# Five modulation units of a two-layer diffusion backbone, moved from TensorE to VectorE dot products

## The reference

```
sh1_l, sc1_l, g1_l, sh2_l, sc2_l, g2_l = split(silu(c)     @ w_ada + b_ada, 6)
sh1_c, sc1_c, g1_c, sh2_c, sc2_c, g2_c = split(silu(c_ctx) @ w_ada + b_ada, 6)
h  = rms_norm(x, norm1_g) * (1 + sc1) + sh1
... = h @ w_in          # attention (a), conformer convolution, differential attention (d), three gates
y  = sigmoid(g0) * (o_mla @ w_o_mla) + sigmoid(g1) * (o_conv @ w_o_conv) + sigmoid(g2) * (o_diff @ w_o_diff)
x  = x + g1 * (y @ w_out)
h2 = rms_norm(x, norm2_g) * (1 + sc2) + sh2
x  = x + g2 * hier_moe(h2)
```

## Time and profile before

| what | us |
|---|---|
| three runs | 1578.43, 1573.87, 1580.1 (median 1578.43) |
| profiled execution, its own time | 1578.7 |
| span from first to last instruction | 1576.9 |
| TensorE busy | 1469.0 (93%) |
| VectorE busy | 629.4 (40%) |
| ScalarE busy | 385.1 (24%) |
| GpSimd busy | 143.1 (9%) |
| mean granted TensorE clock | 0.975 of full speed |

### The profile page before, as it was taken

The page is one execution under the profiler, slowest core; times in us unless marked ns, Lnnn a source line. Parts: engine busy times, 40 slices in busy tenths (PEclk is TensorE's granted clock), DMA queues, the critical chain, the costliest instruction groups (busy, mean ns, idle before and its releaser), DMA issues.

```text
span 1576.9 us, 19712 instructions
## 1 busy us (share of the span) xinstructions
PE 1469.0 (93%) x7940; PEld 825.3 (52%) x7940; DVE 629.4 (40%) x1461; ACT 385.1 (24%) x827; POOL 143.1 (9%) x104
## 2 busy tenths in 40 slices
PE   5999999999999999989997879999999999899886
PEld 3443344454445445565553447644768876555552
DVE  2468943533234202433211117794543214233223
ACT  4111404432222102222221124231542203011111
POOL 0001510000002010002221110051000110000000
PEclk9999999999999999999999899999999999899998
DMA  9422422112221306089999988452212538699994
GB/s 382 178 107 111 190 107 107 54 54 107 104 110 63 163 41 271 37 325 416 418 418 420 411 308 360 194 213 107 101 60 107 218 130 334 262 420 420 420 418 195
DMA packets 49038, 349.23 MB, mean 221 GB/s; under 512 B 7968, under 2 KB 8480, under 8 KB 17328
## 3 DMA queue, kind: packets, MB, share of 16 engines
q1 hardware_dynamic: 43344, 337.42, 53.0%
q0 software_dynamic: 5024, 8.40, 1.4%
q10 hardware_dynamic: 576, 2.10, 0.3%
HBM read 345.00 MB, written 11.80 MB: 226 GB/s over the span
## 4 chain that ended last, share of the span: by engine, by line
PE 80%; DMA 9%; DVE 4%; SPq 3%; ACT 3%; issue 1%; DVEq 0%; POOLq 0%; ACTq 0%
PE bank L358 76%; DMA arena<-w_up_in 7%; ACT arena L1089 2%; PE bank L647 2%; SPq L2425 1%; SPq L2436 1%; DVE arena L1501 1%; PE bank L432 1%; DMA arena<-w_down_in 1%; DMA arena<-ada_in 1%; SPq L2445 1%; PE bank L984 1%; DMA x<-x_in 0%; DVE arena L1745 0%; DMA arena<-y 0%
## 5 line engine op out<-in xcount | busy, mean ns | idle before, releaser
L358 PE MATMUL bank<-arena 128*128 128x512 f32 (+10 forms) x6104 | 1272.6, 453 | 53.9 <-DMA arena<-w_up_in 22.0
L358 PEld LDWEIGHTS bank<-arena 128*128 128x128 f32 (+4 forms) x6104 | 671.0, 162 | 568.0 <-issue 411.1
L1089 ACT ACTIVATE arena<-bank 128x512 f32<-128x512 f32 (+5 forms) x454 | 221.1, 504 | 1014.7 <-PE bank L358 902.3
L1501 DVE SCALAR_TENSOR_TENSOR arena<-arena,bank 64x256 f32<-64x256 f32 (+2 forms) x121 | 58.0, 480 | 436.6 <-ACT arena L1089 267.7
L1501 DVE SCALAR_TENSOR_TENSOR arena<-arena,vec 128x512 f32<-128x512 f32 (+1 forms) x254 | 173.4, 755 | 0.4
L1763 DVE TENSOR_REDUCE am<-bank 128x1 f32<-128x512 f32 (+1 forms) x96 | 55.5, 599 | 181.1 <-PE bank L358 181.1
L2292 POOL TENSOR_TENSOR arena<-arena 128x512 f32<-128x512 f32 (+1 forms) x32 | 31.9, 997 | 551.7 <-DVE arena L1501 551.7
L1089 ACT ACTIVATE arena<-bank,am 128x512 f32<-128x512 f32 (+1 forms) x96 | 58.6, 613 | 73.1 <-DVE am L1766 73.0
L2331 POOL DMA_INDIRECT y<-arena,routing x33 | 33.4, 1013 | 188.5 <-ACT arena L1089 183.5
L358 PE MATMUL bank<-arena,silz 128*32 128x512 f32 x384 | 46.1, 598 | 4.3 <-DMA arena<-ada_in 4.3
L647 PEld LDWEIGHTS bank<-con,arena 128*128 128x128 f32 x240 | 29.3, 141 | 36.7 <-issue 23.6
(11 more groups left out here) (177 smaller groups left out, 672.8 us busy)
## 6 DMA issues: line engine op xcount, KB each, us to landing
arena<-w_down_in SPq DMA_DIRECT2D x65, 1024.0 KB
arena<-w_gate_in SPq DMA_DIRECT2D x61, 1024.0 KB
arena<-w_up_in SPq DMA_DIRECT2D x61, 1024.0 KB
arena<-ada_in SPq DMA_DIRECT2D x24, 2048.0 KB, 8.4
arena<-mg_in SPq DMA_DIRECT2D x12, 2048.0 KB, 7.8
arena<-mo_in SPq DMA_DIRECT2D x6, 2048.0 KB, 8.2
arena<-glu_in SPq DMA_DIRECT2D x4, 2048.0 KB, 12.8
arena<-out_w_in SPq DMA_DIRECT2D x4, 2048.0 KB, 15.1
```

The source lines that it names most:

```text
L358: return nc.tensor.matmul(out, w, rhs, start=start, stop=stop)
L1089: return nc.scalar.activation(out, in_, fn, **kw)
L1501: return V.scalar_tensor_tensor(out, in0, sc, in1, op0=op0, op1=op1)
```

## The change

The five units that stood among the gates and branches of layer 0 leave the ring and TensorE. Their weights come transposed (`adaT`: 128 output columns on the partitions, 1024 inputs along the row), in ten halves of 1 MB. The halves go by turns to two areas outside the ring: that of the convolution output `cv` and that of the values `vd`. VectorE multiplies each with rows of the activations and sums along the row, four products of 128x1024 to a half. The activation rows are loaded once, spread over 128 partitions, and made into silu by a tanh on ScalarE and a product on VectorE.

Half 0 stands before the wait for `dn`, halves 1 and 2 behind the reciprocal, and the other seven each before a branch tile of the last branch, c = 2 left out. A half's load waits until the half two places ahead of it is done. The last two loads stand behind those of the output weights, and the first expert load behind the last half. ScalarE's copies of g1 wait for the last branch, as they overwrite `vd`.

Also, the first differential unit's merge steps are divided in both layers: 4 of them in layer 0 and 8 in layer 1 come on TensorE before the first `turn`. VectorE's and ScalarE's order stays there.

```
-                if kind not in ("mg0", "mg1", "mg4", "mo2"):
+                if kind not in (("mg0", "mg1", "mg4", "mo2") if l else ("mg0", "mg1", "mo0", "mg2", "mg3", "mo1", "mg4", "mo2", "mg5")):
...
+                row_units = more[:ROW_UNITS]
+                del more[:ROW_UNITS]
...
+                AHEAD = (4, 8)[l]
+                def merge_steps(g, part=None):
+                    r0, r1 = merge_range(l, g)
+                    if part is not None:
+                        r0, r1 = ((r0, r0 + AHEAD), (r0 + AHEAD, r1))[part]
...
                 for u in range(len(DU)):
+                    if u == 0:
+                        merge_steps(len(AU), 0)
                     turn(len(AU) + u, dprob(u)[:, 0], DU[u][2])
...
-                    merge_steps(len(AU) + u)
+                    merge_steps(len(AU) + u, None if u else 1)
...
+                        elif l == 0 and (what, b, c) == ("branch", 0, KD - 1):
+                            act.wait_ge(full["d"], Dn[("branch", l, KD - 1, 0)])
+                            act.wait_ge(rows_loaded, 16)
+                            f(tanh_rows, silu_rows, ACT.Tanh, scale=0.5).then_inc(rows_tanh, 1)
...
+                def ada_half():
+                    i = len(half_done)
+                    la, u, hh = halves[i]
+                    w = grid(half_at[i % 2], 2)
+                    dve.wait_ge(half_ready[i % 2], 16 * (i // 2 + 1))
+                    for m in range(2):
+                        c_ = 4 * u + 2 * hh + m
+                        if product_at[0]:
+                            dve.wait_ge(dve_step, product_at[0])
+                        V.scalar_tensor_tensor(product, w[:, m, :], 1.0, silu_rows[:, 0, :], op0=MUL, op1=MUL,
+                                               accum_out=ada[la][:, c_, 0:1]).then_inc(dve_step, 1)
...
+                        ins = V.scalar_tensor_tensor(w[:, m, :], w[:, m, :], 1.0, silu_rows[:, 1, :], op0=MUL, op1=MUL,
+                                                     accum_out=ada[la][:, c_, 1:2])
...
+                    step(ins)
+                    stt(ada[la][:, c_:c_ + 2, :], ada[la][:, c_:c_ + 2, :], 0.5,
+                        vec_at(la, "b_ada")[:, c_:c_ + 2].unsqueeze(2).to_broadcast([128, 2, 2]), MUL, ADD).then_inc(dve_step, 1)
...
+                    if l == 0 and u == 1:
+                        dve.wait_ge(rows_tanh, 1)
+                        step(stt(silu_rows, tanh_rows, 1.0, silu_rows, ADD, MUL))
...
+                if l == 0:
+                    dve.wait_ge(s["pt_ready"], len(AU) + len(DU))
+                    dve.wait_ge(s["pv_full"], len(AU) // 2 + len(DU))
+                    ada_half()
                 dve.wait_ge(empty["a"], A[("dn", l)])
                 V.reciprocal(P[:, 0, q0:T], P[:, 0, q0:T]).then_inc(s["recip_ready"], 1)
+                if l == 0:
+                    ada_half()
+                    ada_half()
...
                 for c in range(KD):
+                    if l == 0 and c != 2:
+                        ada_half()
                     branch(2, c)
...
+            def half_load(i):
+                if i == 0:
+                    sp.wait_ge(dve_step, silu_done[0])
+                elif i == 1:
+                    sp.wait_ge(S[0]["pv_full"], len(attn_units(0)[0]) // 2 + len(attn_units(0)[1]))
+                else:
+                    sp.wait_ge(dve_step, half_done[i - 2])
+                sp.dma_start(half_at[i % 2], a["adaT"][la, u, hh]).then_inc(half_ready[i % 2], 16)
...
+                    if units[n] == ("mg3", 0, 0):
+                        sp.wait_ge(s["conv_out"], CT)
+                        sp.dma_start(silu_rows..., a["crow"].to_broadcast([128, 2 * D])).then_inc(rows_loaded, 16)
+                    if units[n] == ("mo2", 0, 0):
+                        half_load(0)
```

More of the change, by code:

```diff
@@ L28 @@
 NRING = 3
+ROW_UNITS = 5
 NADA = 12
@@ L197, in build @@
         consts_set = sem("consts_set")
+        rows_loaded, rows_tanh = sem("silu_rows_loaded"), sem("silu_rows_tanh")
+        half_ready = [sem(f"ada_half_ready{b}") for b in range(2)]
         silc_tanh, silc_ready = sem("silc_tanh"), sem("silc_ready")
@@ L300, in build @@
         ring_of = [[(n_ - 3 + i_) % NRING for i_ in range(3)] for n_ in (units_of_0, len(units))]
+        halves = [(la, u, hh) for _, la, u in row_units for hh in range(2)]
+        half_at = [cv.rearrange("p c t -> p (c t)"), vd.rearrange("p c t -> p (c t)")]
+        silu_rows = arena[:, 24816:26864].rearrange("p (v k) -> p v k", v=2)
+        tanh_rows = arena[:, 18672:20720].rearrange("p (v k) -> p v k", v=2)
+        product = PT.rearrange("p c t -> p (c t)")
+        half_done, silu_done = [], []
         def ada_behind(key):
@@ L601, in branch_step @@
                             used((f"mo{b}", l, 0), "d")
-                def merge_steps(g):
-                    for r_ in range(*merge_range(l, g)):
+                AHEAD = (4, 8)[l]
[3 more added lines that the diff above has]
+                        r0, r1 = ((r0, r0 + AHEAD), (r0 + AHEAD, r1))[part]
+                    for r_ in range(r0, r1):
                         b, r = divmod(r_, ALL)
@@ L1130, in row_copies @@
             def row_copies(l, kind, tokens):
+                if (l, kind) == (0, "g1"):
+                    act.wait_ge(empty["d"], Dn[("branch", 0, KD - 1, 2)])
                 for v in tokens:
@@ L1522, in scales @@
             def scales(l, which):
-                dve.wait_ge(empty["d"], max(Dn[("adaT", l, u)] for u in {0: (0, 1, 2, 3), 1: (8, 9), 2: (4, 5)}[which]))
+                for u in {0: (0, 1, 2, 3), 1: (8, 9), 2: (4, 5)}[which]:
+                    if ("ada", l, u) in row_units:
+                        dve.wait_ge(dve_step, half_done[halves.index((l, u, 1))])
+                    else:
+                        dve.wait_ge(empty["d"], Dn[("adaT", l, u)])
                 if which == 2:
@@ L1807, in branch @@
                     give(stt(out, out, 1.0, ps[:, 0:NQ], ADD, MUL))
+                def ada_half():
[9 more added lines that the diff above has]
+                                               accum_out=ada[la][:, c_, 0:1]).then_inc(dve_step, 1)
+                        own[0] += 1
+                        product_at[0] = own[0]
+                        ins = V.scalar_tensor_tensor(w[:, m, :], w[:, m, :], 1.0, silu_rows[:, 1, :], op0=MUL, op1=MUL,
+                                                     accum_out=ada[la][:, c_, 1:2])
+                        if m == 0:
+                            ins.then_inc(dve_step, 1)
+                            own[0] += 1
+                    step(ins)
+                    c_ = 4 * u + 2 * hh
+                    stt(ada[la][:, c_:c_ + 2, :], ada[la][:, c_:c_ + 2, :], 0.5,
+                        vec_at(la, "b_ada")[:, c_:c_ + 2].unsqueeze(2).to_broadcast([128, 2, 2]), MUL, ADD).then_inc(dve_step, 1)
+                    own[0] += 1
+                    half_done.append(own[0])
+                product_at = [0]
                 def merge_tiles(g):
@@ L1839, in _ @@
                     merge_tiles(nA + u)
+                    if l == 0 and u == 1:
+                        dve.wait_ge(rows_tanh, 1)
+                        step(stt(silu_rows, tanh_rows, 1.0, silu_rows, ADD, MUL))
+                        silu_done.append(own[0])
                 out_d(len(DU) - 1)
+                if l == 0:
+                    dve.wait_ge(s["pt_ready"], len(AU) + len(DU))
+                    dve.wait_ge(s["pv_full"], len(AU) // 2 + len(DU))
+                    ada_half()
                 dve.wait_ge(empty["a"], A[("dn", l)])
                 V.reciprocal(P[:, 0, q0:T], P[:, 0, q0:T]).then_inc(s["recip_ready"], 1)
+                if l == 0:
+                    ada_half()
+                    ada_half()
                 for i in range(HD):
@@ L1851, in _ @@
                 for c in range(KD):
+                    if l == 0 and c != 2:
+                        ada_half()
                     branch(2, c)
+                assert len(half_done) == len(halves)
                 ada_finish(("mg5", l, 0))
@@ L2410, in _ @@
                         sp.dma_start(wr, a["router"][0]).then_inc(router_loaded, 16)
+                if l == 0:
+                    for i in range(1, len(halves) - 2):
+                        half_load(i)
                 b_last = Dn[("branch", l, KD - 1, 1)]
@@ L2420, in _ @@
                 sp.dma_start(outw[1].rearrange("p k n -> p (k n)"), a["out_w"][l, 1]).then_inc(s["outw_ready1"], 16)
+                if l == 0:
+                    half_load(len(halves) - 2)
+                    half_load(len(halves) - 1)
+                    sp.wait_ge(dve_step, half_done[-1])
                 def expert_quarters(j, pairs, quarters):
@@ L2611 @@
         "ada": flat(rows(w_ada, KD).reshape(L, 128, KD, NADA, 4, 4, 32).transpose(0, 3, 1, 2, 5, 4, 6), 3),
+        "adaT": flat(A(w_ada).transpose(0, 2, 1).reshape(L, NADA, 2, 2, 128, D).transpose(0, 1, 2, 4, 3, 5), 4),
```

(1 more changed line is left out.)

1 line of the change is left out of this document (added).

## The result

| | before | changed |
|---|---|---|
| median of the runs, us | 1578.06 | 1556.24 |
| lowest to highest | 1573.87 to 1580.1 | 1555.49 to 1556.8 |
| profiled execution, its own time / span | 1578.7 / 1576.9 | 1556.7 / 1554.7 |
| mean granted clock | 0.975 | 0.979 |
| VectorE busy | 629.4 | 683.4 |

A forecast was written before the change was run, and what follows sets the result against it. TensorE was taken as the bound, the path for 80% of the span, with room on VectorE. 12.58 + 1.81 + 1.23 - 0.49 = 15.1 us off 1578.4 gave 1563.5 us, range 1557 to 1574.

The forecast's parts named there:

- The units on TensorE: Layer 0: five modulation units leave TensorE, priced by the starts around them; 12.58 us won.
- Nothing on the path for VectorE: Layer 0: VectorE's ten halves fit in its idle time; cost on the path 0.
- The rooms: Layer 0, before branch 0 of the last branch: cover for VectorE's work is gone from 7.0 us a half.
- The size of a half: VectorE, layer 0: four dot products plus a small scale-and-bias take 5.8 us, bounds 5.3 and 10.5.
- Half rate: Rival: layer 0's VectorE products take 2.35 to 2.56 us each, VectorE bounds, 1586 to 1594 us; chance 0.07.
- The transfers: Layer 0: 1 MB loads land in 5.5 us; nothing is lost up to 11.0 us.
- The start of the differential units: First differential unit: steps ahead fill TensorE's wait, 1.81 us won in layer 0; wait moves in layer 1, 0.5 lost.
- The clock: Layer 0, 388 to 390 us: with the idle stretch filled, 2.4 GHz throughout; 1.23 us won, between 0 and 1.23.

The follow-up runs named there:

- the order that removes it: Changed kernel with VectorE combining branches 3 and 4 of layer 1's first differential unit before the next peaks: 1550.55 us, ratio 0.9816.
- the same added work: Idle matmuls ahead of gate 0 of layer 1's last branch, 1.8 or 4.5 us: kernel before 1575.38 or 1578.04 us, changed kernel 1561.27 or 1563.49 us.
- the products twice: Changed kernel with every half's first product of a column issued three times, eight products for four: 1591.55 us, ratio 1.0072.

## Why the prediction was right, and where it failed

*The units on TensorE*: right, undersized. 12.58 us were taken, 13.7 measured net. The term priced the starts around a unit (1.85 and 0.36 us). From turn to turn, a differential unit with a modulation unit took 10.98 us before and 9.02 after, and the one with the turning 9.74 and 9.24: 1.96 and 0.50. Before:

```profile
413.14 0.60 PE L647 MATMUL bank<-con,arena 128*128 128x128 f32 x4
...
422.26 1.92 PE L358 MATMUL bank<-arena,silz 128*32 128x512 f32 x16
424.12 0.44 PE L647 MATMUL bank<-con,arena 128*128 128x128 f32 x2
...
433.86 0.44 PE L647 MATMUL bank<-con,arena 128*128 128x128 f32 x2
```

after:

```profile
404.92 0.60 PE L664 MATMUL bank<-con,arena 128*128 128x128 f32 x4
...
413.94 0.38 PE L664 MATMUL bank<-con,arena 128*128 128x128 f32 x2
...
423.18 0.38 PE L664 MATMUL bank<-con,arena 128*128 128x128 f32 x2
```

The same matmuls take 9.12 us when a unit follows them (413.14 to 422.26) and 9.02 when none does: 0.10 us ahead of the unit had hidden in the rows before it, and 0.14 ahead of the turning. With 1.96 and 0.50 the term is 13.6. The Trainium skill, TensorEngine Tiling (Array Packing), section "Key Properties", says that a change of the tiling mode drains TensorE; the 0.10 and 0.14 us agree with it, but no run here separates this cause.

*Nothing on the path for VectorE*: right, shown by taking the products away. The rooms were right: 7.1 measured for 7.0. The size of a half came out by luck. A half alone took 4.75 us and not 5.8, but the forecast had nothing for GpSimd's additions, which brought seven of the ten to 5.6 to 6.5 us.

*Half rate*: refuted, 1.15 us a product, where the rival had 2.35 to 2.56. With two float32 streams from SBUF and the accumulator there is no halving. The rule of the Trainium skill that the prediction cites, half throughput for this operation with two non-bf16 SBUF sources, does not hold here.

*The transfers*: right. The halves landed in 5.8 us in the median, 4.7 to 10.7, against the 5.5 taken and the 11.0 allowed; VectorE never waited for one:

```profile
DMA to landing us min/median/max: 4.7/5.8/10.7
```

*The start of the differential units*: layer 0 right (1.81 forecast, 1.8 to 2.0 measured net). Layer 1 right: 0.5 us lost forecast, 0.65 measured in the executions without low clock; that the wait moves behind the combination of branch 3 is shown by the order that removes it.

*The clock*: this step failed. "With the stretch filled I expect 2.4 GHz throughout: 1.23 us won" was the only clock term in the sum; the other low stretches were taken to stay as they were, without a reason, and a low clock at a new place was named only as a sign of being wrong. In the two traces the low clock up to the first experts of layer 1, the experts of layer 0 and the 3.4 us just behind them left out, fell from 15.3 to 8.5 us: 3.4 less in layer 0's attention, 1.7 more in its routing, 3.4 more in layer 1's attention, 8.5 less at its experts. Not all of this is time, as part of it lies in waits. The chain rows show what the clock was worth, 3.4 - 1.4 - 2.8 + 7.2 = 6.4 us, instead of 1.23. The change's own part is 15.8 net in stage 1 less 0.65 in stage 2, 15.1 us; with 0.7 us at the start that makes the 22.2 us between the spans. The forecast's own terms were 13.9. So of the miss (7.1 us by the spans, 6.7 by the medians) 1.2 us are size, 5.2 the clock and 0.7 the start. The range took in that the clock's gain might be absent, not that it might come at other places.

What stays open is why the median over executions keeps part of this. The changed kernel came out 22 us faster twice, though one trace lost 0 and one 3.4 us at the experts. The granted clocks of the single executions point the same way as the two traces: they add up to 37.0 us of low clock in the mean of nine executions of the kernel before and 29.6 in the five of the changed kernel beside them, transfer-bound stages included. Against kernels with the same added work it is 17 or 15 us faster. About 15 us are the change's own, and the rest is where it leaves the later stages in time. What decides in a single execution was not settled.

## What to carry to other kernels

An engine that idles beside a full TensorE can take over a matrix-vector product at no cost, if each piece fits the room before its result is due: reckon that room stretch by stretch, not over the stage, and add what an engine that works beside it takes from it. If work is pulled ahead to fill a wait, follow the banks it fills: the wait moves to whoever empties them, unless that order is changed too. Compare traces stage by stage with the low-clock time taken off, but only where TensorE was busy in it, and test a surprise in an untouched stage by shifting it with idle work before believing or explaining it.

## What the runs showed of the hardware

A product of two SBUF streams on VectorE and an addition on GpSimd that run at once slow each other: 2.28 us for 1.22, and 2.12 for 1.27.

```profile
526.77 1.22 DVE L1848 SCALAR_TENSOR_TENSOR arena<-arena 128x1024 f32<-128x1024 f32 x1
527.00 2.12 POOL L2363 TENSOR_TENSOR arena<-arena 128x512 f32<-128x512 f32 x1 [33.05 <-DVE arena L1526]
...
527.92 2.28 DVE L1852 SCALAR_TENSOR_TENSOR arena<-arena 128x1024 f32<-128x1024 f32 x1
```

The addition ends 1.13 us after the first product, and the second product 1.08 us after the addition: the rows look like taking turns. In the trace without products the eight additions took 1.26 to 1.31 us, and so did the last one here, with no product beside it (1.27). The Trainium skill, GPSIMD Engine Reference, section "Specifications", has it that GpSimd shares its SBUF interfaces with VectorE, with contention where a VectorE instruction has two SBUF inputs, and the rows agree. It cost nothing here, as both had room; with the products twice it did, 6.4 us.

In the two blocks of 32 matmuls with 64 columns at the first experts of layer 1 the granted clock fell 1.0 to 2.6 us after a block's start, while its matmuls were issued without a pause, in some executions and not in others. TensorE had idled 0.86 us before the first block and 1.8 before the second, whether the clock fell or not. At the same place 0, 3.4, 6.8 and 8.5 us were lost, 10.2 in one trace, more than the whole of several tuning steps.
